# An S2 made on VectorE, silu pieces moved behind the convolution, and another order of VectorE's states, in a decoder trunk on one core

## The reference

```python
h = rmsnorm(x, norm_g)
b, c, xa, za, q, k, v, zb, ga, gb = split(h @ w_in)           # widths 1024, v and zb 2048
y_a = (b * (conv3(c * xa) + conv_b) * silu(za)) @ w_a_out      # causal, 3 taps, per channel
o   = retention(rotary(q), rotary(k), v)                       # 4 heads, 256 / 512 wide, chunks of 128
y_b = (rms_per_head(o) * silu(zb)) @ w_b_out
out = rmsnorm(x + (sigmoid(ga) * y_a + sigmoid(gb) * y_b) @ w_o, final_g)
```

## Time and profile before

| | us |
|---|---|
| median of 3 runs | 1384.92 (1384.49 to 1386.84) |
| profiled execution, its own time | 1386.63 |
| its span, first to last instruction | 1384.8 |
| TensorE busy | 1368.2 |
| VectorE busy | 991.4 |
| ScalarE busy | 576.3 |
| GpSimd busy | 391.1 |

### The profile page before, as it was taken

How to read it: one execution, slowest core, us unless ns; L and a number is a source line. 1 busy time by engine, 2 the same in 40 slices (tenths; PEclk the granted TensorE clock), 3 DMA queues, 4 the chain that set the end, 5 groups by cost and what they waited for, 6 DMA issues and landing times.

```text
span 1384.8 us, 15981 instructions
## 1 busy us (share of the span) xinstructions
PE 1368.2 (99%) x6162; PEld 1131.3 (82%) x6162; DVE 991.4 (72%) x946; ACT 576.3 (42%) x777; POOL 391.1 (28%) x278
## 2 busy tenths in 40 slices
PE   9999999999999999999999999999999999999997
PEld 8887888888888888888888888888888778888886
DVE  7897444365565555688888888547776799788887
ACT  7834233222222222333333333338878433433445
POOL 0100222233334444443343444214454000000002
PEclk9999999999999999999999999999999999999999
DMA  9646313322221212245543444558657789945443
GB/s 343 179 158 204 117 50 107 122 76 76 76 76 53 70 61 73 89 142 152 152 134 123 111 135 137 182 192 304 232 200 261 154 319 291 254 173 197 158 86 122
DMA packets 105179, 212.69 MB, mean 154 GB/s; under 512 B 6928, under 2 KB 48016, under 8 KB 100112
## 3 DMA queue, kind: packets, MB, share of 16 engines
q1 hardware_dynamic: 101936, 192.77, 41.3%
q0 software_dynamic: 3024, 18.88, 7.1%
q10 hardware_dynamic: 144, 0.02, 0.0%
HBM read 147.68 MB, written 54.53 MB: 146 GB/s over the span
## 4 chain that ended last, share of the span: by engine, by line
PE 86%; DVE 7%; issue 3%; ACT 2%; DMA 1%; POOL 0%; POOLq 0%; DVEq 0%; ACTq 0%
PE psum L2227 18%; PE psum L2230 18%; PE psum L2229 18%; PE psum L2361 6%; PE psum L2363 6%; PE psum L2362 6%; PE psum L2195 2%; PE psum L2197 2%; PE psum L2198 2%; PE psum L2272 1%; PE psum L2274 1%; PE psum L2273 1%; DVE state L1718 1%; DMA arena<-silu_scratch 1%; ACT state_parts L1160 1%
## 5 line engine op out<-in xcount | busy, mean ns | idle before, releaser
L2227 PE MATMUL psum<-hc,slots 128*128 128x512 f32 x1120 | 436.4, 390 | 0.9
L2230 PE MATMUL psum<-hc,slots 128*128 128x512 f32 x1120 | 435.8, 389 | 0.0
L2229 PE MATMUL psum<-hc,slots 128*128 128x512 f32 x1120 | 435.8, 389 | 0.0
L1001 ACT ACTIVATE slots<-work 128x1024 fp32r<-128x1024 f32 x140 | 148.7, 1062 | 510.3 <-PE psum L2230 415.0
L2227 PEld LDWEIGHTS psum<-hc,slots 128*128 128x128 f32 x1120 | 210.2, 188 | 46.9 <-issue 3.6
L1466 DVE TENSOR_TENSOR slots<-work,slots 128x1024 fp32r<-128x1024 f32 x140 | 185.6, 1326 | 86.8 <-ACT slots L1001 86.8
L2230 PEld LDWEIGHTS psum<-hc,slots 128*128 128x128 f32 x1120 | 210.2, 188 | 43.8
L2229 PEld LDWEIGHTS psum<-hc,slots 128*128 128x128 f32 x1120 | 210.2, 188 | 43.4
L1248 ACT ACTIVATE last_slot<-arena 128x1024 fp32r<-128x1024 f32 x112 | 118.3, 1061 | 169.5 <-PE psum L2363 163.3
L2361 PE MATMUL psum<-last_slot 128*128 128x512 f32 x448 | 175.3, 391 | 3.1 <-DVE last_slot L1740 3.0
L2362 PE MATMUL psum<-last_slot 128*128 128x512 f32 x448 | 174.4, 389 | 0.0
(11 more groups left out here) (185 smaller groups left out, 1824.8 us busy)
## 6 DMA issues: line engine op xcount, KB each, us to landing
work<-w_channel SPq DMA_DIRECT2D x80, 512.0 KB, 3.6
arena<-w_last SPq DMA_DIRECT2D x19, 1024.0 KB, 7.5
qk<-qk_scratch SPq DMA_DIRECT2D x32, 512.0 KB, 3.5
arena<-w_last POOLq DMA_DIRECT2D x9, 1024.0 KB, 11.6
v_raw<-value_scratch SPq DMA_DIRECT2D x32, 256.0 KB, 3.8
arena<-gate_scratch SPq DMA_DIRECT2D x16, 512.0 KB, 7.2
value_c<-w_value SPq DMA_DIRECT2D x10, 512.0 KB, 4.6
rows_of_x<-x_rows SPq DMA_DIRECT2D x8, 512.0 KB, 9.0
```

The costliest lines, as they stand in the source:

```text
L1001: nc.scalar.activation(slots[:, u % SLOTS, 0, :], src, ACT.Copy).then_inc(w_hi, 1)
L2227: nc.tensor.matmul(bank, slot[:, 0, w], x_high, start=product in STARTS and j == 0, stop=False, skip_group_check=True)
L2229: nc.tensor.matmul(bank, slot[:, 0, w], x_low, start=False, stop=False, skip_group_check=True)
L2230: last = nc.tensor.matmul(bank, slot[:, 1, w], x_high, start=False, stop=j == 3, skip_group_check=True)
```

## The change

Four edits. In the value stage VectorE makes the first half of the second group's S2 ahead of `first_add(5)`, and `scaled(3)` goes from u = 12 to u = 19. In the retention new_state(2) goes from the start of step 3 to step 2, ahead of state_low(1) and o_gate(0). The convolution's S2 is made by VectorE in two halves (`conv_s2`, at u = 4 and 6) instead of by a DMA, and product 6 waits for it through `early_summed`; t1(1) and t3(1) are both at u = 5, and S4 is a single accumulating DMA. The stage pieces get a new order: the o21 pieces come first, then o22's first; o22's other three come behind the gates, at u = 33, 35 and 37, and T1, T3 and T2 of RET_OUT move with them.

```diff
+STAGE_ORDER = [("gate11", 0), ("gate11", 1), ("o21", 0), ("o21", 1), ("o21", 2), ("o21", 3), ("o22", 0), ("gate22", 0),
+               ("gate22", 1), ("gate12", 0), ("gate12", 1), ("gate21", 0), ("gate21", 1), ("o22", 1), ("o22", 2), ("o22", 3)]
+STAGE_ORDER += [(f"merge{q}", n) for q in ("11", "22", "12", "21") for n in range(4)]
...
@@ SP, last stage
         stage_gate("11", 1)
-        stage_silu("22", 0)
-        stage_silu("22", 1)
-        stage_silu("22", 2)
+        stage_silu("21", 0)
+        stage_silu("21", 1)
+        stage_silu("21", 2)
         store_mixed("11", C11_TILE)
-        stage_silu("22", 3)
+        stage_silu("21", 3)
         parts_split(CONV_OUT, 5)
-        stage_silu("21", 0)
         sp.wait_ge(last_summed, SUMMED[CONV_OUT, "T4", 1])
         load_conv("d")
-        stage_silu("21", 1)
+        stage_silu("22", 0)
         load_ret("a", 0)
-        stage_silu("21", 2)
+        stage_gate("22", 0)
         load_ret("a", 1)
-        stage_silu("21", 3)
-        stage_gate("22", 0)
+        stage_gate("22", 1)
         parts_split(CONV_OUT, 7)
         load_ret("c", 0)
-        stage_gate("22", 1)
         stage_gate("12", 0)
         stage_gate("12", 1)
         store_mixed("22", V2_TILE)
...
             load_ret("e", c)
         store_mixed("12", V_TILES[CONV_OUT])
+        stage_silu("22", 1)
         sp.wait_ge(mixed_out["12"], 16)
         load_ret("c", 1)
+        stage_silu("22", 2)
         store_mixed("21", KEPT_TILE)
+        stage_silu("22", 3)
@@ GpSimd
         split(CONV_OUT, 1, 3)
-        pool.wait_ge(conv_added["S1"], 16)
-        pool.dma_start(quarter(CONV_OUT, "s"), quarter(CONV_OUT, "e"), accum_op=ALU.add).then_inc(conv_added["S2"], 16)
         pool.wait_ge(conv_in["b"], 16)
         pool.dma_start(quarter(CONV_OUT, "b"), w_last[CONV_OUT, 0], accum_op=ALU.add).then_inc(conv_added["S3"], 16)
         split(CONV_OUT, 6, 3)
-        pool.wait_ge(conv_added["S2"], 16)
-        pool.dma_start(quarter(CONV_OUT, "s"), w_last[CONV_OUT, 1], accum_op=ALU.add).then_inc(conv_added["S2"], 16)
+        pool.dma_start(quarter(CONV_OUT, "s"), w_last[CONV_OUT, 1], accum_op=ALU.add).then_inc(conv_added["S4"], 16)
@@ VectorE, value stage
             if u == 16:
+                value_s2(1, 0)
                 first_add(5)
-                for i in range(2):
-                    value_s2(1, i)
+                value_s2(1, 1)
...
-            if u == 12:
-                scaled(3)
...
             if u == 19:
+                scaled(3)
                 for i in range(2):
                     value_s4(1, i)
@@ VectorE, retention
-            if 1 < s - 1 < UPDATES:
+            if 2 < s - 1 < UPDATES:
                 new_state(s - 1)
...
+            if s == 2:
+                new_state(2)
             if 0 < s - 1 < UPDATES:
                 state_low(s - 1)
@@ VectorE, last stage
+        def conv_s2(i):
+            dve.wait_ge(conv_added["S1"], 16)
+            split(CONV_OUT, 1, 2 * i + 1)
+            early_difference("s", "s", "e", i, ALU.add)
...
-            if 1 <= u <= 6:
-                (conv_t1, conv_t3, conv_t2)[(u - 1) % 3]((u - 1) // 3)
+            if u in (1, 5):
+                conv_t1(u // 4)
+            if u in (2, 5):
+                conv_t3(u // 4)
+            if u in (3, 6):
+                conv_t2(u // 4)
+            if u in (4, 6):
+                conv_s2((u - 4) // 2)
...
-            if u in (11, 12, 15, 16):
-                o_silu("22", (11, 12, 15, 16).index(u))
-            if u in (17, 18, 19, 21):
-                o_silu("21", (17, 18, 19, 21).index(u))
+            if u in (11, 15, 17, 18):
+                o_silu("21", (11, 15, 17, 18).index(u))
...
-            if u in (27, 31, 32, 33):
-                ret_t1((27, 31, 32, 33).index(u))
-            if 34 <= u < 38:
-                ret_t3(u - 34)
-            if 38 <= u < 42:
-                ret_t2(u - 38)
+            if u in (19, 33, 35, 37):
+                o_silu("22", (19, 33, 35, 37).index(u))
+            if u in (21, 27, 31, 32):
+                ret_t1((21, 27, 31, 32).index(u))
+            if u in (33, 34, 36, 38):
+                ret_t3((33, 34, 36, 38).index(u))
+            if u in (35, 37, 39, 40):
+                ret_t2((35, 37, 39, 40).index(u))
```

More of the change, by code:

```diff
@@ L160 @@
 STAGE_TILES = (44, 32, 34)
-STAGE = dict(gate11=0, o22=2, o21=6, gate22=10, gate12=12, gate21=14, merge11=16, merge22=20, merge12=24, merge21=28)
-EARLY_SUMS = [(CONV_OUT, n, i) for i in range(2) for n in ("T1", "T3", "T2")]
+STAGE_ORDER = [("gate11", 0), ("gate11", 1), ("o21", 0), ("o21", 1), ("o21", 2), ("o21", 3), ("o22", 0), ("gate22", 0),
+               ("gate22", 1), ("gate12", 0), ("gate12", 1), ("gate21", 0), ("gate21", 1), ("o22", 1), ("o22", 2), ("o22", 3)]
+STAGE_ORDER += [(f"merge{q}", n) for q in ("11", "22", "12", "21") for n in range(4)]
+STAGE = {name: n for n, name in enumerate(STAGE_ORDER)}
+EARLY_SUMS = [(CONV_OUT, n, i) for i in range(2) for n in ("T1", "T3", "T2", "S2")]
 EARLY_SUMMED = {name: n + 1 for n, name in enumerate(EARLY_SUMS)}
 LAST_SUMS = [(CONV_OUT, "T4", i) for i in range(2)]
-LAST_SUMS += [(RET_OUT, n, i) for n in ("T1", "T3", "T2", "T4") for i in range(4)]
+LAST_SUMS += [(RET_OUT, "T1", i) for i in range(4)]
+LAST_SUMS += [(RET_OUT, n, i) for n, i in (("T3", 0), ("T3", 1), ("T2", 0), ("T3", 2), ("T2", 1), ("T3", 3), ("T2", 2), ("T2", 3))]
+LAST_SUMS += [(RET_OUT, "T4", i) for i in range(4)]
 LAST_SUMS += [(OUTPUT, n, i) for n in ("T1", "T3", "T2") for i in range(2)]
@@ L360, in build @@
     out_in = {r: sem(f"out_in_{r}") for r in ("oa", "ob", "oc", "od", "x11", "x12", "x21", "x22")}
-    conv_added = {n: sem(f"conv_added_{n}") for n in ("S1", "S2", "S3")}
+    conv_added = {n: sem(f"conv_added_{n}") for n in ("S1", "S4", "S3")}
     ret_added = {n: [sem(f"ret_added_{n}{c}") for c in range(2)] for n in ("S1", "S2", "S3")}
@@ L673, in load_stage @@
         def load_stage(what, piece, array):
-            k = STAGE[what] + piece
+            k = STAGE[what, piece]
             if k >= 3:
@@ L700, in store_mixed @@
         def store_mixed(quadrant, tile):
-            sp.wait_ge(stage_used, STAGE["gate" + quadrant] + 2)
+            sp.wait_ge(stage_used, STAGE["gate" + quadrant, 1] + 1)
             sp.dma_start(mixed_d[("11", "22", "12", "21").index(quadrant)], tiles(tile, 4)).then_inc(mixed_out[quadrant], 16)
@@ L1178, in staged @@
         def staged(what, n):
-            act.wait_ge(stage_used, STAGE[what] + n + 1)
+            act.wait_ge(stage_used, STAGE[what, n] + 1)
         def summed_here(group, name, i):
@@ L1187, in conv_parts @@
             elif product == 3:
-                act.wait_ge(conv_added["S2"], 32)
+                act.wait_ge(conv_added["S4"], 16)
                 act.wait_ge(conv_in["od"], 16)
@@ L1194, in conv_parts @@
                 n = {6: 2, 5: 1, 7: 3}[product]
-                act.wait_ge(conv_added[f"S{n}"], 16)
+                if product == 6:
+                    act.wait_ge(early_summed, EARLY_SUMMED[CONV_OUT, "S2", j // 2])
+                else:
+                    act.wait_ge(conv_added[f"S{n}"], 16)
                 act.wait_ge(early_summed, EARLY_SUMMED[CONV_OUT, f"T{n}", j // 2])
@@ L1935, in staged @@
         def staged(what, n, at, op):
-            k = STAGE[what] + n
+            k = STAGE[what, n]
             dve.wait_ge(stage_in[k % 3], 16 * (k // 3 + 1))
@@ L1952, in merge @@
             else:
-                dve.wait_ge(stage_used, STAGE["merge" + quadrant] + n)
+                dve.wait_ge(stage_used, STAGE["merge" + quadrant, n - 1] + 1)
             staged("merge" + quadrant, n, tiles(tile + n // 2 * 2), ALU.add if n % 2 else ALU.mult)
@@ L1968, in difference, with early_difference @@
                 .then_inc(last_summed, 1)
-        def early_difference(dst, left, right, i):
-            nc.vector.tensor_tensor(part(CONV_OUT, dst, i), part(CONV_OUT, left, i), part(CONV_OUT, right, i), ALU.subtract)\
+        def early_difference(dst, left, right, i, op=ALU.subtract):
+            nc.vector.tensor_tensor(part(CONV_OUT, dst, i), part(CONV_OUT, left, i), part(CONV_OUT, right, i), op)\
                 .then_inc(early_summed, 1)
@@ L2000, in ret_t3 @@
         def ret_t3(i):
-            dve.wait_ge(stage_used, STAGE["o22"] + i + 1)
+            dve.wait_ge(stage_used, STAGE["o22", i] + 1)
             summed_here(RET_OUT, "T1", i)
@@ L2031, in out_s1 @@
             split(RET_OUT, 7, 7)
-            dve.wait_ge(stage_used, STAGE["merge12"] + 2 * i + 2)
+            dve.wait_ge(stage_used, STAGE["merge12", 2 * i + 1] + 1)
             difference(OUTPUT, "e", "b", "d", i, ALU.add)
@@ L2043, in out_s4 @@
             split(OUTPUT, 6, 2 * i + 1)
-            dve.wait_ge(stage_used, STAGE["merge21"] + 2 * i + 2)
+            dve.wait_ge(stage_used, STAGE["merge21", 2 * i + 1] + 1)
             difference(OUTPUT, "s", "c", "s", i)
```

## The result

The changed kernel takes 1391.01 us (median of 6 runs, 1389.82 to 1391.62), the kernel before 1385.44 beside it (1384.49 to 1386.84). The ratio is 1.0039, 95% interval 1.0026 to 1.0052: slower by 0.39%. The prediction was 1387.2 with a range of 1379.0 to 1391.0: the side was right (it had been given a chance of 0.37), the time lies on the upper end of the range, 0.01 past it as printed, and the loss is 5.6 us where 2.3 had been forecast. The profiled execution after took 1391.29 (span 1389.5), 4.66 more than the one before.

What follows compares the result with a forecast made beforehand. TensorE, busy 1368.2 of 1384.8 us, was taken as the bound. On the profiled 1386.6, -1.1 - 0.9 - 4.4 + 6.6 + 1.7 = +1.9 gave 1388.5; for the median 1386.8 or 1387.7, predicted 1387.2, range 1379.0 to 1391.0.

Steps and rivals of the forecast that it cites:

- Part 1: Value stage: TensorE's 0.88 us wait for unit 18's low part goes, with lost overlap a gain of 1.1 us.
- Part 2: Retention states: update 3's 1.96 us wait goes, but scores(6)'s qk load bounds the gain; 0.9 us taken.
- zero in the faster runs: Retention: the half clock at 941 may be missing from faster runs, and then the new_state(2) move gains nothing.
- Part 3: Convolution, units 7 to 24: S2 on VectorE removes all five TensorE waits, a gain of 4.4 us, bounds 0 to 4.4.
- Part 4: Behind the convolution: late silu pieces crawl beside POOL's additions; TensorE waits 6.6 us at unit 39, half clock adds 1.7.
- what a second gap lets through: Late silu loads: o22,2's 11.5 us shortened by a gap between two additions, so it lands at 1176.
- third rival: Behind the convolution: additions run until 1183.6, o22,3 lands after 1181.9, a second idle and lower clock; about 1392; 13%.
- first rival: Late silu loads: queues take turns in larger lots, pieces land in time, no wait; 1378.5 to 1379.4 us; 25%.
- narrower range: The forecast itself, a wait of 4.5 to 8.5 us at unit 39: 1385 to 1390 us, 50%.

Runs made afterwards that it cites:

- parts 1 to 3: Changed kernel with the stage pieces, their loads and RET_OUT's T1, T3, T2 back in the old order, against the kernel before: 1381.72 us, ratio 0.9969.
- part 1 alone: Kernel before with only the value-stage edit (S2(1,0) ahead of first_add(5), scaled(3) at u = 19): 1383.76 us, ratio 0.9985.
- part 3 alone: Kernel before with only the convolution's S2 on VectorE, old order of the pieces: 1383.09 us, ratio 0.9984.
- part 4 alone: Kernel before with only the new order of pieces, loads and RET_OUT's T1, T3, T2: 1395.4 us, ratio 1.0069.
- part 2 alone: Kernel before with only new_state(2) moved to step 2: 1385.79 us, ratio 1.0002.
- 4 KB rows: Changed kernel with silu_scratch laid out so a piece is read in 128 rows of 4 KB, not 256 of 2 KB: 1387.63 us, ratio 1.0015 to the kernel before.

## Why the prediction was right, and what was mis-sized

**Part 1: right.** Worked out as -1.1. From the second matmul at 52.65 (before, a timeline row like the one at 53.94) to the last before update 3 are 885.35 us before and 884.29 after: -1.06. The profile hides it, because this execution was 1.29 later at 53.94 by waits ahead of the edit. The same count is 884.20 and 884.22 in the profiles of parts 1 to 3 and of part 1 alone, and 885.30 to 885.50 in those of the three parts that leave the value stage as it was. In the runs it is worth 0.15%, 2.1 us with an interval of 0.7 to 3.5, which holds 1.1.

**Part 2: mechanism right, size too large.** The bound named was the qk load, and the waits that replace the long one came as said. I took 0.9 for it. Counting from the last matmul before update 3 to unit 7, a clock of 1.00 gives 147.52 with the long wait (1085.80 - 938.28, part 3 alone) and 147.42 with the short ones (after): 0.1 us. Only where the half clock follows is there more to gain: 147.88 before, 0.46. The other profiles agree: 147.53 with the long wait at full clock (part 1 alone), 147.87 with it and the half clock (part 4 alone), 147.46 with the short ones (part 2 alone). The qk load explains it. scores(6) starts 10.31 us behind that last matmul before, 9.30 after, and 9.26 with the long wait at full clock (947.54 in part 3 alone): the wait hides wholly behind the load, and what reached scores(6) was the half clock. About half of that 1.01 was lost again along the retention (0.50 left at the start of scores(26), 1039.52 before and 1039.25 after); why is not shown. Run by itself the part gave 1.0002. The prediction kept "zero in the faster runs" as its alternative; that was the right one.

**Part 3: mechanism right, size 4.4 only in the profiled execution.** There it is 4.36. But the same 17 units, their code unchanged, take 48.5 us and not 50.6 in the profiles of part 1 alone and part 2 alone (1085.37 to 1133.88 in the latter): how long they wait differs from one profile to another. The wait of 0.53 at unit 8 is not there in either, and the one of 1.51 is 0.78 and 0.21; what makes the difference is not shown. Against 46.2 that leaves 2.3, and part 3 alone measured 0.9984, 2.2 us. This term was taken from one execution as if all had it. The prediction also put five waits into this stretch; they are four, 2.75 us in all, and the fifth is the 0.2 at the kernel's end.

**Part 4: right in mechanism, place and order, a little short in size.** Predicted landing and use, then measured: o22,1 1162, 1162.06; c1 1168.5, 1168.64 (ScalarE's wait for w_last ends there); o22,2 1176, 1176.57; low(39) done 1179.5, 1180.07; wait 6.6, measured 7.27 and 7.43 with its overlap; half clock 1.7, measured 1.82. One term was lucky: the 1176 for o22,2 is 1168.5 + 11.5 less 4 us for "what a second gap lets through", which nothing sized. No gap is needed. Each engine has 32 packets of the additions (4 x 8), and q1 has 16 + 8 + 16 = 40 up to the end of o22,2, so one for one the additions run out first, and the piece lands as they end. An estimate from the packets' own work: 1150.1 + 32 x 0.63 + 32 x 0.09 + 8 x 0.31 = 1175.6, measured 1176.57. With 4 KB rows q1 has 24 turns and needs no more of the additions than that: 1148.8 (their first packet there) + 24 x 0.63 + 16 x 0.18 (a 4 KB packet taken as two of 2 KB) + 8 x 0.31 = 1169.3, measured 1168.95. With part 4 alone, whose additions begin at 1152.3, the first sum gives 1177.8, measured 1179.74.

The third rival's mechanism was half there: the additions' 20 us of work were spread over 25.6 us (1150.1 to 1175.7), because their packets take turns too; the trace of before had already shown it, 27.5 us from 1157.2. It didn't decide, since they began where the forecast had put them (1149.6), not later, and so ended at 1175.7 and not at 1183.6. But it was near: o22,3 landed at 1181.3 (28.1 us behind its issue), where 1181.9 was named as the limit; low(41) was done at 1185.7, when unit 41 (1187.4) was not waiting for it. In the medians the part alone is 1.0069, 9.6 us with an interval of 6.8 to 12.5, against 8.3; on top of parts 1 to 3 it is 1.0070 (1.0039 / 0.9969).

**The first rival fell.** It stood on turns in larger lots, the rule of 9 to 17 descriptors to a turn in the Trainium skill's "DMA: Bandwidth & Descriptors", section on queues, rings and completion order. The counts after are 66 to 65 in 3 us, 121 to 129 and 128 to 126 in 6 us, with 4 KB rows 112 to 113, and the landings fit the count of single turns above. By the rule o22,1's 16 packets an engine would have passed in a turn or two, and they trickled through for over 10 us; in this case the measurement decides against the rule.

**The sum.** Of the medians' 5.6 us, 2.3 were forecast. The missing 3.3 are, of the terms above, 2.2 of part 3, 0.8 of part 2 (about half of its 0.9 stood in the final number, and +0.3 was measured), 1.3 of part 4, less 1.0 of part 1, all within the runs' intervals but part 3's (1.0 to 3.5 us of gain, 4.4 forecast); so the mis-sized step is part 3's gain, read from one profile that lost 2.1 us more than two others of the same code. The forecast's own narrower range, 1385 to 1390, was missed by this.

## What to carry to other kernels

A load that is cheap alone is priced, beside accumulating DMAs on another queue, by the packets of it and of all that stands ahead of it on its queue, each of which waits a turn; so longer rows, or a place ahead of the additions, matter more than its bytes. Count the packets of both queues per engine first: the one with fewer is through first. A gain worked out from chained waits in one profile should be checked against how much the same stretch varies between executions before it is set against a loss. And when a late piece is mended, look at once for the next piece's deadline.

## What the runs showed of the hardware

A low clock after an idle is not given by the idle alone. Before, and with part 4 alone, 1.96 us of idle at update 3 were followed by a granted clock of 0.51 to 0.57 from 941 on; with part 1 alone and part 3 alone the same idle, 1.96 and 1.97 us, left it at 1.00. Behind 7.27 us (after) and 6.94 us (part 4 alone) it fell both times, and behind 4.17 us too (4 KB rows). What such a stretch cost depended on how much of it TensorE still spent idle: 6.8 us at 0.50 (after) cost unit 39 1.82 us, because the first half of it lay in the wait, and 3.4 us at 0.50 wholly in work cost unit 41 1.72 (4 KB rows: 4.44 us to the next unit and not 2.72).

An accumulating DMA slows down beside plain ones as they do beside it. The four of 1 MB in the changed kernel landed in 11.9, 15.4, 12.5 and 11.8 us while pieces and weights were queued. The S2 addition of the kernel before took 8.2 us for 1 MB while the other queue had 2.9% of the engines (1078.7 to 1087). A quarter of the bytes did not land in a quarter of the time: 256 KB took 8.3 us. A weight load of 1 MB took 17.0 us behind a piece and beside the additions, and 7.1 when these were a quarter as large.
